# mLSTM denominators in a hybrid-layer kernel: per-tile ones products replaced by a GpSimd sum of the weights and one ones product per head

## The reference, cut to what matters

```
s_qk = jnp.einsum('bhld,bhsd->bhls', qj, kj) * w_intra
num = jnp.einsum('bhls,bhse->bhle', s_qk, vj) + w_inter[..., None] * jnp.einsum('bhld,bhde->bhle', qj, C)
den = jnp.sum(s_qk, axis=-1) + w_inter * jnp.einsum('bhld,bhd->bhl', qj, n)
hj = num / jnp.maximum(jnp.abs(den), jnp.exp(-m_row))[..., None]
```

## Time and profile before

| | us |
|---|---|
| median of 3 runs | 2657.06 (2655.26 to 2662.62) |
| the profiled execution, its own time | 2657.8 |
| its span in the trace | 2656.0 |
| TensorE busy | 2407.6 (91%) |
| VectorE busy | 1133.7 (43%) |
| ScalarE busy | 957.1 (36%) |
| GpSimd busy | 813.5 (31%) |
| mean granted TensorE clock | 0.951 of full |
| the mLSTM stage, first layer, 195.0 to about 263.9 | 69 |
| the mLSTM stage, second layer, 904.5 to about 971.8 | 67 |

### The profile page before, as it was taken

The page is one execution under the profiler, slowest core; times in us unless marked ns, Lnnn a source line. Parts: engine busy times, 40 slices in busy tenths (PEclk is TensorE's granted clock), DMA queues, the critical chain, the costliest instruction groups (busy, mean ns, idle before and its releaser), DMA issues. The chain is left out here.

```text
span 2656.0 us, 39964 instructions
## 1 busy us (share of the span) xinstructions
PE 2407.6 (91%) x16798; PEld 1888.8 (71%) x16798; DVE 1133.7 (43%) x1917; ACT 957.1 (36%) x1387; POOL 813.5 (31%) x364
## 2 busy tenths in 40 slices
PE   5998999997989989999878979997799998999987
PEld 3884776775868756768757757885576676888865
DVE  2626284334055253842331566674244445305222
ACT  3331455443143314453342333332446514222232
POOL 1430333231433213333223322220332333444432
PEclk8998999997999989999989989998899999999989
DMA  3220222221222102222112200000321213222321
GB/s 121 96 76 5 87 72 72 71 72 34 77 91 95 48 33 71 80 72 72 56 51 97 87 17 4 4 4 2 97 72 60 68 64 103 96 95 96 101 74 64
DMA packets 50145, 176.37 MB, mean 66 GB/s; under 512 B 5604, under 2 KB 6188, under 8 KB 49964
## 3 DMA queue, kind: packets, MB, share of 16 engines
q1 hardware_dynamic: 49404, 172.78, 19.5%
q10 hardware_dynamic: 560, 1.00, 0.1%
HBM read 171.65 MB, written 2.11 MB: 65 GB/s over the span
## 5 line engine op out<-in xcount | busy, mean ns | idle before, releaser
L302 POOL TENSOR_TENSOR w_low<-work,w_high 128x1024 fp32r<-128x1024 f32 x310 | 748.8, 2416 | 1559.6 <-ACT w_high L265 1559.6
L248 PE MATMUL ps<-x_high_tiles,w_high 128*128 128x512 f32 x1560 | 635.6, 407 | 62.9 <-DVE x_low_tiles L326 45.7
L248 PE MATMUL ps<-x_low_tiles,w_high 128*128 128x512 f32 x1592 | 629.8, 396 | 0.0
L248 PE MATMUL ps<-x_high_tiles,w_low 128*128 128x512 f32 x1560 | 616.9, 395 | 0.0
L265 ACT ACTIVATE w_high<-work 128x1024 fp32r<-128x1024 f32 x310 | 327.8, 1058 | 797.2 <-PE ps L248 784.7
L248 PE MATMUL ps<-arena_parts,w_high 128*128 128x512 f32 x1280 | 402.7, 394 | 25.5 <-DVE arena_parts L326 22.1
L248 PEld LDWEIGHTS ps<-x_high_tiles,w_high 128*128 128x128 f32 x1560 | 298.4, 191 | 163.4 <-issue 93.0
L248 PEld LDWEIGHTS ps<-x_low_tiles,w_high 128*128 128x128 f32 x1592 | 305.5, 192 | 63.8 <-issue 4.1
L248 PEld LDWEIGHTS ps<-x_high_tiles,w_low 128*128 128x128 f32 x1560 | 298.7, 191 | 65.1
L248 PEld LDWEIGHTS ps<-arena_parts,w_high 128*128 128x128 f32 x1280 | 242.4, 190 | 79.5 <-DVE arena_parts L326 23.8
L248 PE MATMUL ps<-arena_parts,w_low 128*128 128x512 f32 x656 | 257.1, 392 | 0.0
(11 more groups left out here) (361 smaller groups left out, 2766.1 us busy)
## 6 DMA issues: line engine op xcount, KB each, us to landing
work<-w_first SPq DMA_DIRECT2D x180, 512.0 KB, 3.6
work<-w_second SPq DMA_DIRECT2D x134, 512.0 KB, 3.5
xT_sb<-xT SPq DMA_DIRECT2D x8, 256.0 KB, 6.6
outT<-arena SPq DMA_DIRECT2D x8, 256.0 KB, 2.2
arena<-distance_bias SPq DMA_DIRECT2D x4, 256.0 KB, 3.7
small<-small SPq DMA_DIRECT2D x1, 819.5 KB, 4.8
arena<-consts SPq DMA_DIRECT2D x1, 544.0 KB, 5.6
base<-consts ACTq DMA_DIRECT2D x1, 512.0 KB, 5.8
```

Of the source, the lines that this page charges most:

```text
L248: ins = pe.matmul(out, lhsT, rhs, start=(n == 0 and k == 0 and q == 0), stop=(n == unit["granules"] - 1 and k == len(ops) - 1 and q == 2))
L302: pool.tensor_tensor(m.wl[:, g % NSPLIT, :], m.raw[:, g % NRAW, :], m.wh[:, g % NSPLIT, :].bitcast(F32), ALU.subtract).then_inc(sem["low_r ...
```

## The change: where the denominators are summed

The product with ones at line 706 goes from every step. POOL now keeps a running total of the weights of a head, in `m.ml_total`: a copy in a head's first step, an addition in the others, on the same 512, 384, 256 and 128 columns. It has two buffers, for even and odd heads. TensorE multiplies the total by the ones once per head, over all 512 columns, in `denominator(h)`. For heads 0 to 2 this stands in TensorE's stream where the ones product of the next head's first step stood, behind its numerator products; for head 3 at the end. DVE's `finish(h)` waits for it (`den_done`). Before it writes the weight of step n, DVE now waits for the numerator products and for the total of step n - 2, in place of `pv_done`. The low parts of the next stage's weights (`parts`) stand in POOL's stream behind the addition of step 5.

```
+        def parts(pool):
             for g in range(NSPLIT):
                 pool.wait_ge(sem["high_ready"], g + 1)
                 pool.tensor_tensor(m.wl[:, g, :], m.raw[:, g, :], m.wh[:, g, :].bitcast(F32), ALU.subtract).then_inc(sem["low_ready"], 1)
+        @block.gpsimd
+        def _(pool):
+            for n, (h, j) in enumerate(steps):
+                total, w = m.ml_total[:, h % 2, j * P:S], m.tmp[:, 2 + n % 2, 0:S - j * P]
+                pool.wait_ge(sem["w_ready"], n + 1)
+                if j == 0:
+                    if h >= 2:
+                        pool.wait_ge(sem["den_done"], h - 1)
+                    pool.tensor_copy(total, w).then_inc(sem["w_summed"], 1)
+                else:
+                    pool.wait_ge(sem["w_summed"], n)
+                    pool.tensor_tensor(total, total, w, ALU.add).then_inc(sem["w_summed"], 1)
+                if n == 5:
+                    parts(pool)
...
+            def denominator(h):
+                pe.wait_ge(sem["w_summed"], T * (h + 1))
+                if h:
+                    pe.wait_ge(sem["den_read"], h)
+                pe.matmul(m.ps[:, 5, :], m.ones, m.ml_total[:, h % 2, :], start=True, stop=True).then_inc(sem["den_done"], 1)
...
                 if h and j == 0:
-                    pe.wait_ge(sem["den_read"], h)
-                pe.matmul(m.ps[:, 5, j * P:S], m.ones, w, start=(j == 0), stop=(j == T - 1)).then_inc(sem["pv_done"], 1)
+                    denominator(h - 1)
+            denominator(ML_H - 1)
...
             def finish(h):
                 dve.wait_ge(sem["em_copied"], h + 1)
-                dve.wait_ge(sem["pv_done"], T * (h + 1))
+                dve.wait_ge(sem["den_done"], h + 1)
...
                 if n >= 2:
-                    dve.wait_ge(sem["pv_done"], n - 1)
+                    dve.wait_ge(sem["num_done"], n - 1)
+                    dve.wait_ge(sem["w_summed"], n - 1)
```

More of the change, by code:

```diff
@@ L652, in mlstm_stage @@
     em = ab
-    with stage(nc, "rows_ready", "qk_ready", "arg_ready", "exp_ready", "w_ready", "num_done", "pv_done", "num_copied", "den_read",
+    with stage(nc, "rows_ready", "qk_ready", "arg_ready", "exp_ready", "w_ready", "num_done", "w_summed", "den_done", "num_copied", "den_read",
                "raw_loaded", "high_ready", "low_ready",
@@ L663, in _ @@
             sp.wait_ge(sem["raw_loaded"], 16 * len(ahead))
-        @block.gpsimd
-        def _(pool):
+        def parts(pool):
             for g in range(NSPLIT):
@@ L2057, in build @@
         m.ml_squares = arena[:, 28:30, :]
+        m.ml_total = arena[:, 25:27, :]
         m.gate_a = m.pick[32:48, :]
```

## The result

| | before | after |
|---|---|---|
| median, us | 2656.16 (4 runs) | 2682.22 (4 runs, 2679.01 to 2685.83) |
| ratio to before | | 1.0096, 95% interval 1.0076 to 1.0116 |
| ratio in a second measurement | | 1.0085, 1.0072 to 1.0099 |
| the profiled execution, its own time | 2657.8 | 2685.83 |
| its span | 2656.0 | 2684.0 |

The change costs some 24 us. I had forecast +14 and a range up to 2678: the direction was right, the size too small and the range missed.

The account below looks back on a forecast made before the run. TensorE and DVE were taken to bound the mLSTM stage in turns; waits, saved products, the lifted hold and clock summed to +6.3 and +8.0 us by layer, +14.3 in all, giving a 2671.3 us median, range 2663 to 2678.

Parts of the forecast that it names:

- What bounds, and the wait: mLSTM stage: TensorE and DVE alternate as bound; finish waits for the new denominator product, +3.6 us three times a layer.
- the sum: All terms over both mLSTM stages: +6.3 us in the first layer, +8.0 in the second, together +14.3.
- Ones products that go: TensorE's path in the mLSTM stage loses ones products: -1.94 us in head 0, -1.08 each in heads 1 and 2.
- GpSimd: mLSTM stage: GpSimd keeps up with its totals, 0; line 634 is no longer held by the low parts, -1.59 us.
- The tight place: Step 8: DVE needs step 6's total, which stands behind the low parts; it just fits, 0, up to +2.4 us.
- the second rival: GpSimd gets in the way: low parts delay step 6 or 7's mask, step 8 2.4 us later per layer; 2676.1, chance 0.15.
- TensorE's clock: Behind longer gaps before line 689 and in head 3, half clock for 5.2 us; head 3 +0.5 first layer, +2.2 second.
- What the mLSTM stage gains or loses, the program gains or loses: Because barriers close all stages, the mLSTM stage's change passes to the program, twice; no size for other stages.
- the prediction's own sign: Check on the trace: the forecast is wrong if the difference lies outside the two mLSTM stages, forecast 6 and 8 us longer.

Follow-up runs that it names:

- e1: Changed kernel with the denominators' one product moved up, right behind its own head's last numerator products; 2649.77 us, ratio 0.9986.
- e2: Kernel before with one wait added: finish of heads 0 to 2 also waits for the next head's first-step numerator products; 2671.86 us, ratio 1.0061.
- e9: Changed kernel with TensorE filler: five 128-row products in heads 1 and 2, 15 products of 256 columns in head 3; 2664.03 us, ratio 1.0016.
- e11: Kernel before with 128-row filler alone: three products in head 1, one in head 2, seven of 256 columns in head 3; 2651.31 us, ratio 0.9973.
- e16: Changed kernel with a second DVE reciprocal at the mLSTM stage's end, making the stage 3.4 us longer; 2688.87 us, ratio 1.0117.
- e6: Changed kernel with TensorE filler: five more 4-row products in heads 1 and 2, 15 products of 256 columns in head 3; 2680.35 us, ratio 1.0077.

## Why the prediction was wrong in size

- **What bounds, and the wait.** Right. Three waits a layer, line 765 starting 3.54 us later behind line 785 than before (214.47 - 209.99 against 213.21 - 212.27), where the sum had 3.6. e1 takes the wait away and with it the loss; e2 adds a wait of 2.7 to the kernel before and loses 16.
- **Ones products that go.** In the second layer head 0 came out at 1.94 as reckoned: from the first exponents to the weight of step 4 it took 15.90 before and 13.96 after. In the first it was 0.96, because TensorE was at half clock for longer at the stage's start (granted 0.59 over 192.3 to 200.7, and 0.80 over as long from the stage's start before, 194.1 to 202.5). The sum had no term for this.
- **GpSimd.** Right in the changed kernel: no wait on it, the copy 0.61 us (taken as 1.27), the mask held for 816 ns at most (292 in the median), line 634 back at 1.29. The Trainium skill's rule (GPSIMD Engine Reference, section Specifications), that GpSimd contends with VectorE instructions that have two SBUF inputs, agrees with the trace: of VectorE's instructions in this stage only the mask lengthened. (The others do not all read PSUM, as I wrote: the reciprocal of line 630 reads SBUF, but with one input, and kept its 3.35 us beside the low parts.) The tight place was real and came out once TensorE was quicker (2.37 us in e1). In e9, at full clock, head 1 takes 229.54 - 210.53 = 19.01 from weight to weight; in e11 it takes 228.79 - 212.53 = 16.26. That is +2.75, where the terms without clock and GpSimd have 3.6 - 1.59 - 1.08 = +0.93. So the second rival's mechanism is there, at some 1.8 us a layer, and in the changed kernel the slow products behind the gap hide it.
- **TensorE's clock: the term that was mis-sized.** I took half clock for 5.2 us behind each gap; it lasted 6.6 to 6.8 (0.52 over 221.25 to 228.00, 0.50 over 241.36 to 248.00). From the start of line 709 to the next head's weight I had 8.2; it was 230.10 - 221.25 = 8.85 and 250.39 - 241.36 = 9.03. By heads in the first layer: -0.96, +1.51, +3.96, +4.26, in all +8.8 for +6.3. In the second: -1.94, +1.00, +3.90, +5.91, in all +8.9 for +8.0. (A slip beside it: head 3 at full clock is 3.9 + 0.4 = 4.3 against 4.72, so -0.4 and not -0.3.) Over four traces on each side the two stages grew by 16.6 where the sum had 14.3, so this term alone would have left the result inside the range.
- **"What the mLSTM stage gains or loses, the program gains or loses": the step that failed.** I had put the stages that no edit touches at nothing, in the sum and in the range, with the barriers as the only reason. The barriers hold the order, not the length. Of the timed 22.6 to 25.5 us the mLSTM stages account for 16.6. The stages behind them account for 4.6: 385.3 every time now, which is 5.9 above the mean of before in the first layer and 1.2 below it in the second. Some 3 remain, about the 3.5 of the RWKV stages' means. By the prediction's own sign, that the forecast is wrong "if the difference lies outside these two stages", a third of it does.

What stays open: why the stages behind always have the same length in the changed kernel. Five of before's eight are at 385.3 or more too, so if each were dealt by chance at that rate, eight of eight would come about 2 times in 100 (estimate, from before's eight stages, and the two layers are not alike in before). A start 3.4 us later (e16) did not change them; holding the clock up to the end (e6's and e9's first stages) brought 382.3 and 383.8, not 379. For the RWKV stage, four traces on each side do not tell the 3.5 from chance. A better forecast of the range would have carried the scatter of the untouched stages, 376.6 to 387.0 and 271.8 to 280.9, which two or three traces of before would have shown.

## What to carry to other kernels

Before a product is cut from a busy engine, look at who waits for its result: four products in four places gave the last one early, one product, standing behind work that waits for another engine, gave a wait of 3.5 us to an engine that was itself on the path. Moving that one product per head was worth 22 us of stage time, more than all the products that were saved. And a longer gap on TensorE is paid twice, as the gap and as slow products behind it; price both (here the clock is at least 2.1 of the 8.3 us by which a stage grew). And take several traces of the unchanged kernel before a range is stated: stages that no edit touches scattered here by 10 us, and went into the difference.

## What was not expected of the hardware

- Repeated products with 4 rows kept TensorE busy through the gap, but its clock fell during them in head 1 (12 passes in 8.04 us; 5.41 in head 2) and behind them everywhere. Products with 128 rows in the same gaps ran at full clock in all four places (10 passes in 4.45 us), the clock fell behind them in three and for a shorter time, and with them the changed kernel lost 4 us instead of 24.
- The same stage of 1732 matmul passes takes 376.6 to 387.0 us in traces of one kernel, with DVE and ACT busy times alike to 0.2 us; only the granted clock differs (0.95 to 0.98).
- A GpSimd copy of 128x512 takes 0.61 us, under half of the addition of the same size (1.27).
